# Conformer's last slice: two of its four blocks convolved by diagonal matmuls on TensorE, with the layer norm sums of the first three slices taken in the meantime

## The chip, the cores and the metric

The kernel runs as one program on one core of a Trainium2 chip. The metric is the device time of one execution in microseconds (us). The time of the kernel before is the median of 3 runs.

## The reference, cut to what matters

The model is a trunk of two layers over 256 tokens of width 2048 (batch 1). Layer 0 mixes tokens with a gated DeltaNet, layer 1 with a Conformer convolution module; each layer then applies a SwiGLU FFN. The change lies wholly in the Conformer module of layer 1:

```
def conformer_conv(h, pw1_w, pw1_b, dw_w, dw_b, ln_w, ln_b, pw2_w, pw2_b):
    u = h @ pw1_w + pw1_b                    # 2048 -> 4096
    a, gate = jnp.split(u, 2, axis=-1)
    u = a * jax.nn.sigmoid(gate)             # GLU, 2048 channels
    u = depthwise_conv(u, dw_w) + dw_b       # width 31, centred, over the 256 tokens
    u = jax.nn.silu(layernorm(u, ln_w, ln_b))# over the 2048 channels, LN_EPS = 1e-5
    return u @ pw2_w + pw2_b
```

`layernorm` subtracts the mean over the 2048 channels of a token, divides by the root of the mean square of what is left (plus LN_EPS), and applies a weight and a bias for each channel.

## The kernel before, in words

Each engine has its own instruction list, written out by hand (a `@block` function for each), and semaphores order the engines among themselves. No planner is involved: an instruction runs when those before it on its engine have been issued and its `wait_ge` is met.

**Layout.** In the Conformer the channels lie on the 128 partitions: the 2048 channels are 16 blocks (`kc`, KC = 16) of 128, the 256 tokens (T) lie along the free dimension. The work goes in four slices `n` of four blocks each. `glu` holds the four blocks of one slice after the GLU; `dwo` (a view of the buffer `y`, so rows of the profile call it y) holds all 16 blocks after the depthwise convolution. `psg`, `pst` and `psn` are PSUM buffers of 4, 2 and 2 banks.

**First projection (pw1).** TensorE multiplies the raw float32 weights (`tile32`, L630) for the two halves of a slice. ScalarE copies each half out of PSUM (`half`, L1915), TensorE transposes it (`turn2`, L620, called at L988 to L997), ScalarE takes the sigmoid (`sigm`, L1921), VectorE multiplies (`unit`, L1502). ScalarE has nothing else to do here: in this stage no weights are split. DMA brings one weight tile of 1 MB after the other into four slots.

**Depthwise convolution.** VectorE does it alone (`dw`, L1508 to L1526): 31 taps (`TAPS_V`, the centre tap first), for each tap one instruction for each of the four blocks. The first tap is a TENSOR_SCALAR with the bias (L1520), the 30 others are SCALAR_TENSOR_TENSOR, `dst = src * w + dst` (L1522). An instruction waits, by the semaphore `tap`, until the one four places before it has completed. The last instruction of a slice raises `dw_ok`. Slices 0 to 2 run in a loop, slice 3 (`dw(3, order)`, L1534) is written out.

**Layer norm.** Everything from here on waits for the fourth slice. TensorE sums over the channels by multiplying with a matrix of ones: 16 matmuls of 128 x 256 (L1004; the 12 of slices 0 to 2 can run early), VectorE divides by D (L1538) and subtracts the mean from all 16 blocks, four at a time (L1543), ScalarE squares four blocks at a time (L1943), TensorE sums the squares (L1009, 16 matmuls), VectorE divides (L1545), ScalarE takes the root (L1945), VectorE the reciprocal (L1547) and multiplies all blocks with it (L1551, four instructions).

**Second projection (pw2).** From here the kernel's matmuls use weights and activations split in a high and a low part: ScalarE makes `whi` (`hi`, L1596), VectorE `wlo` (`lo`, L1033), and `tile` (L643 and L649) does 16 matmuls with `whi` and 8 with `wlo` for a tile. VectorE makes `wlo` of the first two tiles between L1551 and L1556. ScalarE applies silu with weight and bias for each block (L1952) and copies to the high part `h_hi3` (L1956); VectorE subtracts to get the low part `h_lo3` (L1556) in four steps, and raises `pre_lo`, on which the first matmul of pw2 waits. Weights for the next slices of pw2 are loaded once `w_lo` tells that a slot is free. After pw2 come the residual update, the norm, and the FFN of layer 1.

Of the kernel before, what the change touches and what calls it, by code (L numbers as in the profile page):

```python
# [14 lines left out]
P = 128  # L15
D = 2048
T = 256
TT = T // P
KC = D // P
# [9 lines left out]
CTAPS = 31  # L29
TAPS_V = (CTAPS // 2,) + tuple(k for k in range(CTAPS) if k != CTAPS // 2)  # L30
# [4 lines left out]
RMS_EPS, LN_EPS, L2_EPS = 1e-6, 1e-5, 1e-6  # L35
# [29 lines left out]
def build(nc, x_in, c_in, ada_w, ada_b, norm_w, gdn_in_w, gdn_conv_w, gdn_A_log, gdn_dt_bias,  # L65
# [16 lines left out]
    G_P2 = G_P1 + 4 * 8  # L82
# [14 lines left out]
    with stack:  # L97
        def sb(name, shape, dt=F32, at=stack):
            return at.enter_context(nc.sbuf_tensor(name, shape, dt))

        def sem(name):
            return stack.enter_context(nc.semaphore(name))
# [19 lines left out]
        ident = sb("ident", [P, P])  # L122
        ones = sb("ones", [P, P])

        NV_NORM, NV_ADAB, NV_C, NV_CONV, NV_DW, NV_CF = 0, 128, 320, 336, 656, 1152
        vec = sb("vec", [P, 1232])
        V_PW1B, V_DWB, V_LNW, V_LNB = NV_CF, NV_CF + 32, NV_CF + 48, NV_CF + 64
# [94 lines left out]
        p3 = ExitStack()  # L222
        aring3 = sb("aring3", [P, 2, D], at=p3)
        aacc3 = sb("aacc3", [P, 2, D], at=p3)
        h_hi3 = sb("h_hi3", [P, KC, T], F32R, at=p3)
        h_lo3 = sb("h_lo3", [P, KC, T], F32R, at=p3)
        hf3 = sb("hf3", [P, 2, 4, T], at=p3)
# [10 lines left out]
        lnst = sb("lnst", [P, 2, T], at=p4)  # L238
        sg4 = sb("sg4", [P, 4, T], at=p4)
        glu = sb("glu", [P, 4, T], at=p4)  # L240
# [3 lines left out]
        h32 = aring3[:, :, :].rearrange("p a (k t) -> p (a k) t", t=T)  # L244
        pw2b = ev4[:, :, :, :].rearrange("p a t n -> p (a t n)")
        dwo = y[:, :, :].rearrange("p a (k t) -> p (a k) t", t=T)

        psg = stack.enter_context(nc.psum_tensor("psg", [P, 2, TT, NSL], F32))
        pst = stack.enter_context(nc.psum_tensor("pst", [P, 4, T], F32))
        psn = stack.enter_context(nc.psum_tensor("psn", [P, 4, T], F32))  # L250
# [43 lines left out]
        tap = sem("tap")  # L294
# [54 lines left out]

        ln_p, ln_v, ln_s = sem("ln_p"), sem("ln_v"), sem("ln_s")  # L350
        pb_land = sem("pb_land")
        out_sem = sem("out_sem")


# [261 lines left out]
        def _(pe):  # L616
            mm = nc.tensor.matmul
# [376 lines left out]
            with pe.Fori(1, 4) as i:  # L994
                pw1_pair(i, True)
            turn2((ps_read, S_P2), ev4[:, 1], psn, t_g, (sg_ok, 3))
            pe.wait_ge(sg_ok, 4)  # L997
            unsplit[0] = 32

            pe.wait_ge(glu_ok, 4)  # L1000
            for kc in range(KC):
                if kc % 4 == 0 and kc >= 8:
                    pe.wait_ge(dw_ok, kc // 4 + 1)
                i = mm(pst[:, 0, :], ones[:, :], dwo[:, kc, :], start=kc == 0, stop=kc == KC - 1)  # L1004
            i.then_inc(ln_p, 1)
            for q in range(4):
                pe.wait_ge(ln_s, q + 1)
                for j in range(4):
                    i = mm(pst[:, 2, :], ones[:, :], hf3[:, q % 2, j, :], start=q + j == 0, stop=q + j == 6)  # L1009
                i.then_inc(ln_p, 1)  # L1010
            with pe.Fori(0, 2) as i:
                for s in range(2):
                    n = 2 * i + s
                    pe.wait_ge(ps_read, S_P2 + n - 1)
                    for j in range(4):
                        tile(G_P2 + 4 * n + j, (G_P2 + j) % 2, psg[:, (S_P2 + s) % 2], h_hi3, h_lo3,
                             range(4 * j, 4 * j + 4), j == 0, j == 3, ready=(pre_lo, 8 + j + 1))
# [7 lines left out]
        def _(dve):  # L1025
# [482 lines left out]
            def dw(n, part):  # L1508

                for m, k in part:  # L1510
                    off = k - CTAPS // 2
                    a, e = max(0, -off), T - max(0, off)
                    for b in range(4):
                        if m:
                            dve.wait_ge(tap, dwt.at() - 3)
                        w = vec[:, ds(NV_DW + k * KC + 4 * n + b, 1)]
                        src = glu[:, b, a + off:e + off]
                        dst = dwo[:, ds(4 * n + b, 1), a:e].rearrange("p a t -> p (a t)")
                        if m == 0:
# [11 lines left out]
            with dwt.loop(dve, 1, 4, 4 * CTAPS - 1) as i:  # L1531
                pw1_pair(i)
            unit(3)
            dw(3, order)  # L1534

            lv = Tally(ln_v)
            dve.wait_ge(ln_p, 1)
            lv.inc(ts(lnst[:, 0, :], pst[:, 0, :], 1.0 / D, None, MUL))  # L1538
            lv.wait(dve)
            dve.wait_ge(dw_ok, 4)  # L1540
            for q in range(4):
                d4 = dwo[:, 4 * q:4 * q + 4, :]
                lv.inc(tt(d4, d4, lnst[:, 0:1, :].broadcast_to([P, 4, T]), SUB))  # L1543
            dve.wait_ge(ln_p, 5)
            lv.inc(ts(lnst[:, 1, :], pst[:, 2, :], 1.0 / D, LN_EPS, MUL, ADD))  # L1545
            dve.wait_ge(ln_s, 5)
            lv.inc(nc.vector.reciprocal(lnst[:, 1, :], lnst[:, 1, :]))  # L1547
            lv.wait(dve)
            for q in range(4):
                d4 = dwo[:, 4 * q:4 * q + 4, :]  # L1550
                lv.inc(tt(d4, d4, lnst[:, 1:2, :].broadcast_to([P, 4, T]), MUL))  # L1551
            for j in range(2):
                lo(G_P2 + j, G_P2 + j)
            for q in range(4):
                dve.wait_ge(ln_s, 5 + 2 * (q + 1))
                tt(h_lo3[:, 4 * q:4 * q + 4, :], hf3[:, q % 2], h_hi3[:, 4 * q:4 * q + 4, :].bitcast(F32),  # L1556
                   SUB).then_inc(pre_lo, 1)
            dve.wait_ge(pb_land, 16)

            def y_bias(n, par):  # L1560
# [27 lines left out]
        def _(act):  # L1588
# [37 lines left out]
            def pre(n, hi_, hfb, low0):  # L1626
                act.wait_ge(aff_ok, n + 1)

                def odd(q):

                    act.wait_ge(pre_tr, 4 * n + q + 1)
                    if q == 3 and hi_ is not None:
                        act.wait_ge(pre_lo, low0 + 2)
                    for j in range(4):
                        kc = 4 * q + j
                        i = av(hfb[:, kc, :] if hi_ is None else hfb[:, 1, j, :], psn[:, j, :], ACT.Identity, bias=mod[:, 3 * n, kc:kc + 1],
                               scale=aff[:, n, kc:kc + 1])
# [12 lines left out]
                odd(3)  # L1650
                high(3)
# [254 lines left out]
            ffn(0, G_F0, S_F0)  # L1906
            squares(2, lambda t: (x_up, 3 + t))
            pre(2, None, h32, 8)

            def half(n, which):  # L1910

# [24 lines left out]
            sigm(3)  # L1936
            hi(G_P2, G_P2)
            hi(G_P2 + 1, G_P2 + 1)
            for q in range(4):
                act.wait_ge(ln_v, 2 + q)  # L1940
                if q >= 2:
                    act.wait_ge(ln_p, q)
                av(hf3[:, q % 2], dwo[:, 4 * q:4 * q + 4, :], ACT.Square).then_inc(ln_s, 1)  # L1943
            act.wait_ge(ln_v, 6)
            av(lnst[:, 1, :], lnst[:, 1, :], ACT.Sqrt).then_inc(ln_s, 1)  # L1945
            for q in range(4):
                act.wait_ge(ln_v, 8 + q)
                if q >= 2:
                    act.wait_ge(pre_lo, 8 + q - 1)
                for j in range(4):  # L1950
                    kc = 4 * q + j
# [195 lines left out]
```

## Time and profile before

| | |
|---|---|
| median of 3 runs | 3355.26 us (3352.37 to 3358.61) |
| the profiled execution, its own time | 3356.01 us |
| its span | 3354.4 us |
| mean granted TensorE clock | 0.947 of full speed |
| busy: TensorE matmul / weight load | 2975.1 us (89%) / 2390.3 us (71%) |
| busy: VectorE | 2319.3 us (69%) |
| busy: ScalarE | 1255.6 us (37%) |
| busy: GpSimd | 249.6 us (7%) |

The profile describes one execution. PE is TensorE's matmul and PEld its weight load, DVE is VectorE, ACT is ScalarE, POOL is GpSimd, SP is the engine that issues most DMAs. L12 is line 12 of the kernel. A float32 matmul shows as two records: the 12 early matmuls of L1004 are 24 of them. The record of a matmul runs on beyond the start of the next one, so what a stream of them costs is read from the time of the whole stream and its count. The granted clock (PEclk) is 1.00 at 2.4 GHz and 0.50 at 1.2 GHz.

### The profile page before, as it was taken

The page shows a single profiled execution, that of the slowest core. Times are in us where ns is not written, and L with a number is a line of the kernel's source. Part 1 is how long each engine was busy: PE and PEld are TensorE (multiplying, and loading weights), DVE is VectorE, ACT ScalarE, POOL GpSimd, SP SyncE. Part 2 cuts the span into 40 slices and gives each one's busy share as a digit, 9 for nine tenths or more (in the row PEclk, how much of TensorE's full clock was granted, in tenths as well). Part 3 has the DMA queues.
Part 4 walks back from the last instruction along what each step waited for, and adds up shares of the span by engine and source line. Part 5 has one row for each costly group of instructions (what it writes and reads, how often), then busy time and mean ns, then how long its engine had stood idle before and what let it go on. Part 6 is the DMA issues. An engine that isn't in the chain of part 4 may idle for free.

```text
span 3354.4 us, 37695 instructions
## 1 busy us (share of the span) xinstructions
PE 2975.1 (89%) x13446; PEld 2390.3 (71%) x13446; DVE 2319.3 (69%) x2367; ACT 1255.6 (37%) x1143; POOL 249.6 (7%) x266
## 2 busy tenths in 40 slices
PE   1599999997778599799999999799757999999998
PEld 1578878876667478688888888644346788888886
DVE  7588868976767377787877878529965655565555
ACT  0256644334454433433333333301134433333333
POOL 0011111323333100000000000000000000000000
PEclk9899999998999699899999999899878999999998
DMA  9467766664332299688978888354324666665663
GB/s 361 179 225 239 241 211 230 204 221 140 97 97 82 56 382 361 250 315 315 343 291 313 329 317 333 122 163 151 113 74 164 238 201 204 214 206 201 201 212 125
DMA packets 322154, 731.34 MB, mean 218 GB/s; under 512 B 48129, under 2 KB 64337, under 8 KB 293649
## 3 DMA queue, kind: packets, MB, share of 16 engines
q1 hardware_dynamic: 316256, 709.85, 60.0%
q0 software_dynamic: 5808, 20.35, 1.8%
q8 instruction: 50, 0.82, 0.1%
q14 instruction: 40, 0.32, 0.0%
HBM read 710.45 MB, written 19.69 MB: 218 GB/s over the span
## 4 chain that ended last, share of the span: by engine, by line
PE 78%; DVE 11%; ACT 4%; DMA 3%; issue 3%; DVEq 1%; SPq 0%; POOL 0%; ACTq 0%; POOLq 0%
PE psg L643 43%; PE psg L649 21%; PE psg L630 5%; DVE y L1522 2%; DMA aring<-in_ada_w 2%; PE pst L809 1%; PE psn L670 1%; DVE exb L1373 1%; PE pst L620 1%; ACT dec L1790 1%; DMA wraw<-in_gdn_out_w 1%; DVE wlo L1033 1%; DVE aacc L1137 1%; PE psn L620 1%; PE pst L802 1%
## 5 line engine op out<-in xcount | busy, mean ns | idle before, releaser
L1033 DVE TENSOR_TENSOR wlo<-wraw,whi 128x2048 fp32r<-128x2048 f32 x409 | 937.2, 2292 | 488.2 <-ACT whi L1596 486.4
L1596 ACT ACTIVATE whi<-wraw 128x2048 fp32r<-128x2048 f32 x409 | 783.5, 1916 | 1307.4 <-PE psg L649 1201.5
L643 PE MATMUL psg<-whi,h_hi 128*128 128x512 f32 (+1 forms) x2336 | 742.2, 400 | 35.5 <-DVE h_lo L1556 13.0
L643 PE MATMUL psg<-whi,h_lo 128*128 128x512 f32 (+1 forms) x2336 | 731.4, 395 | 0.0
L649 PE MATMUL psg<-wlo,h_hi 128*128 128x512 f32 (+1 forms) x2336 | 582.6, 393 | 12.1 <-DVE wlo L1033 12.1
L643 PEld LDWEIGHTS psg<-whi,h_hi 128*128 128x128 f32 x2336 | 445.2, 194 | 130.2 <-issue 21.0
L649 PEld LDWEIGHTS psg<-wlo,h_hi 128*128 128x128 f32 x2336 | 443.0, 191 | 104.8 <-DVE wlo L1033 13.8
L643 PEld LDWEIGHTS psg<-whi,h_lo 128*128 128x128 f32 x2336 | 449.1, 193 | 94.1
L1043 DVE SCALAR_TENSOR_TENSOR aacc<-aring,cond,aacc 128x2048 f32<-128x2048 f32 x151 | 354.2, 2345 | 6.7 <-DMA aring<-in_ada_w 6.0
L630 PE MATMUL psg<-wraw,aring 128*128 128x512 f32 x512 | 221.1, 592 | 0.0
L643 PE MATMUL psg<-whi,g_hi 128*128 128x512 f32 x704 | 219.9, 394 | 0.0
L643 PE MATMUL psg<-whi,g_lo 128*128 128x512 f32 x704 | 219.4, 393 | 0.0
L1522 DVE SCALAR_TENSOR_TENSOR y<-glu,vec,y 128x241 f32 (+29 forms) x480 | 186.4, 462 | 0.0
L630 PEld LDWEIGHTS psg<-wraw,aring 128*128 128x128 f32 x512 | 96.7, 190 | 118.6 <-issue 118.6
L649 PE MATMUL psg<-wlo,g_hi 128*128 128x512 f32 x704 | 173.9, 389 | 0.0
L2079 POOL DMA_DIRECT2D d_cw<-cwc x4 | 4.7, 1172 | 2123.1 <-DVE cwc L1117 2123.1
L643 PEld LDWEIGHTS psg<-whi,g_hi 128*128 128x128 f32 x704 | 134.1, 191 | 28.0
L643 PEld LDWEIGHTS psg<-whi,g_lo 128*128 128x128 f32 x704 | 133.9, 190 | 28.2
L1441 DVE TENSOR_TENSOR y<-psg,y 128x1024 f32<-128x1024 f32 x88 | 107.5, 1222 | 66.9 <-PE psg L649 65.7
L649 PEld LDWEIGHTS psg<-wlo,g_hi 128*128 128x128 f32 x704 | 132.2, 188 | 27.5
L1236 DVE SCALAR_TENSOR_TENSOR cv<-pst,vec,cv 128x254 f32<-128x254 f32 (+1 forms) x256 | 117.2, 480 | 25.1 <-DVE cv L1234 0.2
L670 PE MATMUL psn<-ones,aacc 128*128 128x1 f32 x384 | 57.9, 285 | 81.5 <-DVE aacc L1137 48.6
(216 smaller groups left out, 2650.7 us busy)
## 6 DMA issues: line engine op xcount, KB each, us to landing
aring<-in_ada_w SPq DMA_DIRECT2D x192, 1024.0 KB, 7.0
wraw<-in_ffn_in_w SPq DMA_DIRECT2D x176, 1024.0 KB, 6.8
wraw<-in_gdn_in_w SPq DMA_DIRECT2D x97, 1024.0 KB, 5.2
wraw<-in_ffn_out_w SPq DMA_DIRECT2D x88, 1024.0 KB, 5.4
wraw<-in_cf_pw_w SPq DMA_DIRECT2D x48, 1024.0 KB, 5.3
wraw<-in_gdn_out_w SPq DMA_DIRECT2D x32, 1024.0 KB, 8.8
wraw<-d_rr SPq DMA_DIRECT2D x16, 1024.0 KB, 5.1
x<-in_x SPq DMA_DIRECT2D x2, 2048.0 KB, 9.9
```

The source lines that it names most:

```text
L620: return nc.tensor.transpose(dst, src, ident[:, :])
L630: i = mm(ps[:, t, :], a[:, kc, t * P:(t + 1) * P], wraw[:, slot, j * NSL:(j + 1) * NSL], start=first and j == 0, stop=last and j == len(kc ...
L643: mm(ps[:, t, 0:width], a[:, kc, t * P:(t + 1) * P], wh, start=first and j + n == 0, stop=False)
L649: i = mm(ps[:, t, 0:width], a_hi[:, kc, t * P:(t + 1) * P], wl, start=False, stop=last and j == len(kcs) - 1)
L670: i = mm(psn[:, 0, kc:kc + 1], acc[:, kc * P:(kc + 1) * P], ones[:, 0:1], start=True, stop=True)
L802: i = mm(ps_a[:, c, :], t64[:, q, c, t, :], rv[:, q, o, c, :], start=True, stop=True)
L1033: tt(wlo[:, j % 2, :], wraw[:, j % 4, :], whi[:, j % 2, :].bitcast(F32), SUB).then_inc(w_lo, 1)
L1043: stt(acc, ring[:, par, :], c, acc, MUL, ADD).then_inc(a_used, 1)
L1236: i = stt(dst, src, w, dst, MUL, ADD)
L1441: tt(yj, psg[:, (s0 + par) % 2], yj, ADD).then_inc(ps_read, 1)
L1522: i = stt(dst, src, w, dst, MUL, ADD)
L1596: av(whi[:, j % 2, :], wraw[:, j % 4, :], ACT.Copy).then_inc(w_hi, 1)
```

## The change

- A buffer `diag` of 2 x 32 matrices of 128 x 128 floats, laid over `h_hi3` and `h_lo3`, which are unused between the FFN of layer 0 and pw2. ScalarE fills 62 of them right after the input of the Conformer module is normed (`pre(2, ...)`): the identity times a column of tap weights, for the 31 taps of blocks 14 and 15.
- Slice 3 on VectorE (`dw_last`) does only blocks 12 and 13: 62 instructions where there were 124, each waiting for the one two places before. Blocks 14 and 15 are convolved on TensorE: 62 float32 matmuls of a diagonal matrix with `glu` shifted by the tap, accumulated in two banks of `psn`; ScalarE takes them out with the bias.
- TensorE takes the 12 mean sums of slices 0 to 2 before the diagonal matmuls, as soon as `dw_ok` reaches 3, so it no longer waits for the last GLU there. After tap 16 VectorE computes from them a provisional mean over 1536 channels (`mean0`) and subtracts it from the 12 blocks, then finishes the taps and subtracts it from the other four. ScalarE squares the first three slices during the taps, TensorE sums their squares after the diagonal matmuls, then sums the four blocks of slice 3 and its squares.
- The mean of the shifted blocks is now that of slice 3's four blocks divided by D (those of the first three slices sum to nought after the shift). The variance is the mean square of the shifted values less the square of that mean (`dev2`). The mean is subtracted (`center`) together with the scaling, block group by block group.
- `lo` of the first pw2 tile moves ahead of the wait for TensorE's blocks; that of the second behind the first `h_lo3` step.

```diff
@@ tensor @@
             turn2((ps_read, S_P2), ev4[:, 1], psn, t_g, (sg_ok, 3))
+            unsplit[0] = 32
+            pe.wait_ge(dw_ok, 3)
+            for kc in range(12):
+                i = mm(psg[:, 0, 0, 0:T], ones[:, :], dwo[:, kc, :], start=kc == 0, stop=kc == 11)
+            i.then_inc(ln_p, 1)
             pe.wait_ge(sg_ok, 4)
-            unsplit[0] = 32
-
             pe.wait_ge(glu_ok, 4)
-            for kc in range(KC):
-                if kc % 4 == 0 and kc >= 8:
-                    pe.wait_ge(dw_ok, kc // 4 + 1)
-                i = mm(pst[:, 0, :], ones[:, :], dwo[:, kc, :], start=kc == 0, stop=kc == KC - 1)
-            i.then_inc(ln_p, 1)
-            for q in range(4):
+            pe.wait_ge(diag_ok, 1)
+            for m, k in enumerate(TAPS_V):
+                off = k - CTAPS // 2
+                a, e = max(0, -off), T - max(0, off)
+                for b in range(2):
+                    i = mm(psn[:, 2 * b, a:e], diag[:, b, m, :], glu[:, 2 + b, a + off:e + off], start=m == 0, stop=m == CTAPS - 1)
+            i.then_inc(dwp_done, 1)
+
+            def square_sums(q):
                 pe.wait_ge(ln_s, q + 1)
                 for j in range(4):
-                    i = mm(pst[:, 2, :], ones[:, :], hf3[:, q % 2, j, :], start=q + j == 0, stop=q + j == 6)
+                    i = mm(psg[:, 1, 1, 0:T], ones[:, :], lnsq[:, q, j * T:(j + 1) * T], start=q + j == 0, stop=q + j == 6)
                 i.then_inc(ln_p, 1)
+            for q in range(3):
+                square_sums(q)
+            pe.wait_ge(ln_v, 6)
+            for j in range(4):
+                i = mm(psg[:, 1, 0, 0:T], ones[:, :], dwo[:, 12 + j, :], start=j == 0, stop=j == 3)
+            i.then_inc(ln_p, 1)
+            square_sums(3)
@@ vector @@
-            dw(3, order)
+            def dw_last(part):
+                for m, k in part:
...
+                    for b in range(2):
+                        if m:
+                            dve.wait_ge(tap, dwt.at() - 1)
...
             lv = Tally(ln_v)
+            mean0, dev2 = sg4[:, 0:1, :], sg4[:, 1, :]
+            def shift(k0, n):
+                lv.inc(tt(dwo[:, k0:k0 + n, :], dwo[:, k0:k0 + n, :], mean0.broadcast_to([P, n, T]), SUB))
+            dw_last(order[:16])
             dve.wait_ge(ln_p, 1)
-            lv.inc(ts(lnst[:, 0, :], pst[:, 0, :], 1.0 / D, None, MUL))
+            lv.inc(ts(sg4[:, 0, :], psg[:, 0, 0, 0:T], 1.0 / (12 * P), None, MUL))
             lv.wait(dve)
+            for q in range(3):
+                shift(4 * q, 4)
+            dw_last(order[16:])
             dve.wait_ge(dw_ok, 4)
+            shift(12, 2)
+            lo(G_P2, G_P2)
+            dve.wait_ge(dwp_ok, 1)
+            shift(14, 2)
+            dve.wait_ge(ln_p, 5)
+            lv.inc(ts(lnst[:, 0, :], psg[:, 1, 0, 0:T], 1.0 / D, None, MUL))
+            lv.wait(dve)
+            lv.inc(tt(dev2, lnst[:, 0, :], lnst[:, 0, :], MUL))
+            lv.wait(dve)
+            lv.inc(ts(dev2, dev2, -1.0, LN_EPS, MUL, ADD))
...
+            center(0)
+            dve.wait_ge(ln_p, 6)
+            lv.wait(dve)
+            lv.inc(stt(lnst[:, 1, :], psg[:, 1, 1, 0:T], 1.0 / D, dev2, MUL, ADD))
             dve.wait_ge(ln_s, 5)
             lv.inc(nc.vector.reciprocal(lnst[:, 1, :], lnst[:, 1, :]))
             lv.wait(dve)
-            for q in range(4):
-                d4 = dwo[:, 4 * q:4 * q + 4, :]
-                lv.inc(tt(d4, d4, lnst[:, 1:2, :].broadcast_to([P, 4, T]), MUL))
-            for j in range(2):
-                lo(G_P2 + j, G_P2 + j)
+            scale(0)
+            for q in range(1, 4):
+                center(q)
+                lv.wait(dve)
+                scale(q)
...
+            low(0)
+            lo(G_P2 + 1, G_P2 + 1)
+            for q in range(1, 4):
+                low(q)
@@ scalar @@
             pre(2, None, h32, 8)
+            for b in range(2):
+                for m, k in enumerate(TAPS_V):
+                    c = NV_DW + k * KC + 14 + b
+                    i = av(diag[:, b, m, :], ident[:, :], ACT.Copy, scale=vec[:, c:c + 1])
+            i.then_inc(diag_ok, 1)
...
-            for q in range(4):
+            def square(q):
+                av(lnsq[:, q, :], dwo[:, 4 * q:4 * q + 4, :].rearrange("p k t -> p (k t)"), ACT.Square).then_inc(ln_s, 1)
+            for q in range(3):
                 act.wait_ge(ln_v, 2 + q)
-                if q >= 2:
-                    act.wait_ge(ln_p, q)
-                av(hf3[:, q % 2], dwo[:, 4 * q:4 * q + 4, :], ACT.Square).then_inc(ln_s, 1)
+                square(q)
+            act.wait_ge(dwp_done, 1)
+            for b in range(2):
+                i = av(dwo[:, 14 + b, :], psn[:, 2 * b, :], ACT.Identity, bias=vec[:, V_DWB + 14 + b:V_DWB + 15 + b])
+            i.then_inc(dwp_ok, 1)
             act.wait_ge(ln_v, 6)
+            square(3)
+            act.wait_ge(ln_v, 11)
             av(lnst[:, 1, :], lnst[:, 1, :], ACT.Sqrt).then_inc(ln_s, 1)
             for q in range(4):
-                act.wait_ge(ln_v, 8 + q)
+                act.wait_ge(ln_v, 13 + 2 * q)
```

`center(q)` subtracts the mean from four blocks and `scale(q)` multiplies them by the reciprocal root; each is one VectorE instruction of 128 x 1024.

## Rows read from the trace of the kernel before

**Rows 1.** The page: the chain that ended last, shares by engine and line.
```profile
PE 78%; DVE 11%; ACT 4%; DMA 3%; issue 3%; DVEq 1%; SPq 0%; POOL 0%; ACTq 0%; POOLq 0%
```

**Rows 2.** That chain in order of time, 2402 to 2520: start, length, what (xcount).
```profile
2404.49 1.67 DVE glu L1502 x4
2406.19 1.38 DVE y L1520 x4
2407.57 46.51 DVE y L1522 x120
2454.12 3.70 PE pst L1004 x8
...
2459.57 1.07 ACT hf L1943
2460.67 8.88 PE pst L1009 x32
2469.57 0.44 DVE lnst L1545
2470.03 0.42 ACT lnst L1945
2470.48 1.76 DVE lnst L1547
2472.27 4.63 DVE y L1551 x4
2476.90 4.40 DVE wlo L1033 x2
2481.30 1.15 DVE h_lo L1556
...
2482.58 6.56 PE psg L643 x16
2489.14 1.81 PE psg L649 x8
2490.96 3.63 PE psg L643 x16
```

**Rows 3.** Timeline of PE around the last GLU: start, length, group, [idle before <-releaser].
```profile
2401.33 1.09 PE L620 MATMUL psn<-ident,ev 128*128 128x128 f32 x8 [1.11 <-ACT ev L1915]
2406.30 7.11 PE L1004 MATMUL pst<-y,ones 128*128 128x256 f32 x24 [3.88 <-DVE glu L1502]
```

**Rows 4.** Windows: length, busy (xcount) of PE, PEld, DVE, ACT, POOL, then PEclk, DMA.
```profile
2406.00:2410.00 4.00, 3.70 (x9) 3.00 (x10) 3.96 (x12) 1.62 (x1) 0.00 (x0) 0.57 0.29 121
2410.00:2414.00 4.00, 3.40 (x16) 2.66 (x14) 4.00 (x12) 0.00 (x0) 0.00 (x0) 1.00 0.00 0
```

**Rows 5.** Timeline of PE elsewhere: small float32 matmuls, and the pause before one group.
```profile
1109.72 2.92 PE L893 MATMUL psn<-wraw,dec 128*128 128x128 f32 x24 [0.84 <-DVE og L1366]
2109.07 3.62 PE L670 MATMUL psn<-ones,aacc 128*128 128x1 f32 x32
804.38 1.16 PE L809 MATMUL pst<-yh,dec 128*128 128x128 f32 x8 [2.03 <-ACT yh L1781]
```

**Rows 6.** Window just after that pause, same columns as Rows 4.
```profile
806.00:808.00 2.00, 2.00 (x8) 1.36 (x7) 1.97 (x4) 0.00 (x0) 2.00 (x3) 0.50 0.01 4
```

**Rows 7.** Timeline of ACT: before pw1, and the operations that the change's new ones resemble.
```profile
2156.57 0.20 ACT L1624 ACTIVATE st<-st 128x2 f32<-128x2 f32 x1
2174.39 1.93 ACT L1636 ACTIVATE aring<-psn,mod,aff 128x256 f32<-128x256 f32 x4 [1.18 <-PE psn L620]
2201.85 1.02 ACT L1915 ACTIVATE ev<-psg 128x1024 f32<-128x1024 f32 x1 [25.54 <-PE psg L630]
2473.53 2.08 ACT L1952 ACTIVATE hf<-y,vec 128x256 f32<-128x256 f32 x4 [1.78 <-DVE y L1551]
```

**Rows 8.** Timeline of PE: the transposes that use the first half of pw1.
```profile
2208.52 1.04 PE L620 MATMUL pst<-ident,ev 128*128 128x128 f32 x8
```

**Rows 9.** Timeline of DVE: a conv chain waiting tap by tap; a 512 element add.
```profile
291.84 3.92 DVE L1236 SCALAR_TENSOR_TENSOR cv<-pst,vec,cv 128x254 f32<-128x254 f32 x8
2511.53 1.28 DVE L1563 TENSOR_TENSOR y<-psg,ev 128x512 f32<-128x512 f32 x2
```

More of the change, by code:

```diff
@@ L224, in build @@
         aacc3 = sb("aacc3", [P, 2, D], at=p3)
+        p3d = ExitStack()
+        diag = sb("diag", [P, 2, 32, P], at=p3d)
+        p3d.close()
         h_hi3 = sb("h_hi3", [P, KC, T], F32R, at=p3)
@@ L246, in build @@
         dwo = y[:, :, :].rearrange("p a (k t) -> p (a k) t", t=T)
+        lnsq = aacc3[:, :, :].rearrange("p a (q n) -> p (a q) n", q=2)
         psg = stack.enter_context(nc.psum_tensor("psg", [P, 2, TT, NSL], F32))
@@ L351, in build @@
         pb_land = sem("pb_land")
+        diag_ok, dwp_done, dwp_ok = sem("diag_ok"), sem("dwp_done"), sem("dwp_ok")
         out_sem = sem("out_sem")
@@ L1533, in _ @@
             unit(3)
-            dw(3, order)
+            def dw_last(part):
+                for m, k in part:
+                    off = k - CTAPS // 2
+                    a, e = max(0, -off), T - max(0, off)
+                    for b in range(2):
+                        if m:
+                            dve.wait_ge(tap, dwt.at() - 1)
+                        w = vec[:, NV_DW + k * KC + 12 + b:NV_DW + k * KC + 13 + b]
+                        src, dst = glu[:, b, a + off:e + off], dwo[:, 12 + b, a:e]
+                        if m == 0:
+                            i = ts(dst, src, w, vec[:, V_DWB + 12 + b:V_DWB + 13 + b], MUL, ADD)
+                        else:
+                            i = stt(dst, src, w, dst, MUL, ADD)
+                        if m == CTAPS - 1 and b == 1:
+                            i.then_inc(dw_ok, 1)
+                        else:
+                            dwt.inc(i)
@@ L1540, in _ @@
+            dw_last(order[16:])
             dve.wait_ge(dw_ok, 4)
-            for q in range(4):
+            shift(12, 2)
+            lo(G_P2, G_P2)
+            dve.wait_ge(dwp_ok, 1)
+            shift(14, 2)
+            assert lv.n == 6
+            dve.wait_ge(ln_p, 5)
[4 more added lines that the diff above has]
+            lv.inc(ts(dev2, dev2, -1.0, LN_EPS, MUL, ADD))
@@ L1542, in _, with center, scale @@
+            def center(q):
                 d4 = dwo[:, 4 * q:4 * q + 4, :]
                 lv.inc(tt(d4, d4, lnst[:, 0:1, :].broadcast_to([P, 4, T]), SUB))
-            dve.wait_ge(ln_p, 5)
-            lv.inc(ts(lnst[:, 1, :], pst[:, 2, :], 1.0 / D, LN_EPS, MUL, ADD))
+            def scale(q):
+                d4 = dwo[:, 4 * q:4 * q + 4, :]
+                lv.inc(tt(d4, d4, lnst[:, 1:2, :].broadcast_to([P, 4, T]), MUL))
+            center(0)
+            dve.wait_ge(ln_p, 6)
+            lv.wait(dve)
@@ L1546, in _ @@
+            lv.inc(stt(lnst[:, 1, :], psg[:, 1, 1, 0:T], 1.0 / D, dev2, MUL, ADD))
+            assert lv.n == 11
             dve.wait_ge(ln_s, 5)
@@ L1548, in _, with low @@
             lv.wait(dve)
-            for q in range(4):
-                d4 = dwo[:, 4 * q:4 * q + 4, :]
-                lv.inc(tt(d4, d4, lnst[:, 1:2, :].broadcast_to([P, 4, T]), MUL))
-            for j in range(2):
-                lo(G_P2 + j, G_P2 + j)
-            for q in range(4):
+            scale(0)
[3 more added lines that the diff above has]
+                scale(q)
+            def low(q):
                 dve.wait_ge(ln_s, 5 + 2 * (q + 1))
@@ L1938, in _ @@
             hi(G_P2 + 1, G_P2 + 1)
-            for q in range(4):
+            def square(q):
+                av(lnsq[:, q, :], dwo[:, 4 * q:4 * q + 4, :].rearrange("p k t -> p (k t)"), ACT.Square).then_inc(ln_s, 1)
+            for q in range(3):
                 act.wait_ge(ln_v, 2 + q)
-                if q >= 2:
-                    act.wait_ge(ln_p, q)
-                av(hf3[:, q % 2], dwo[:, 4 * q:4 * q + 4, :], ACT.Square).then_inc(ln_s, 1)
+                square(q)
[3 more added lines that the diff above has]
+            i.then_inc(dwp_ok, 1)
             act.wait_ge(ln_v, 6)
+            square(3)
+            act.wait_ge(ln_v, 11)
             av(lnst[:, 1, :], lnst[:, 1, :], ACT.Sqrt).then_inc(ln_s, 1)
             for q in range(4):
-                act.wait_ge(ln_v, 8 + q)
+                act.wait_ge(ln_v, 13 + 2 * q)
                 if q >= 2:
```

## The prediction

> **What bounds the kernel now.** I read the page's chain of waits first, then that chain in order of time, then the timelines of the engines and the windows with the granted clock. Over the whole span TensorE carries 78% of the chain and VectorE 11% [rows 1]. Around the change it is the other way round. From the last GLU (2404.49) to the first matmul of pw2 (2482.58) lie 78.1 us, in which VectorE's 120 tap instructions alone hold 46.51 us; then come four mean sums (3.70), the subtraction, squares and their sums (8.88), root and reciprocal, the scaling (4.63), two weight splits (4.40) and the first low part (1.15) [rows 2]. TensorE does 12 early sums at 2406.30 and then has nothing until 2454.12 [rows 2, 3]. After 2482.58 the chain is TensorE, tile by tile (3.63 + 1.81 us), so I take what the first pw2 matmul gains as a gain of the whole kernel, all later work keeping its distance to it.
>
> **Where the 12 sums go.** They now wait for slice 2, not for the last GLU. TensorE's transposes end at 2402.42 [rows 3] and VectorE leaves slice 2 just before it starts the GLU at 2404.49 [rows 2]; I take 2404.45. The stream of 24 records took 7.11 us [rows 3], of which the first part ran at clock 0.57 and the rest at 1.00 [rows 4]. At full clock 16 records take 3.40 us, 0.2125 each [rows 4], and 24 would take 5.10. Whether the clock still falls when TensorE pauses 2.0 us instead of 3.88 is open. After a pause of 2.03 us elsewhere it did fall: the granted clock was 0.50 right after [rows 5, 6]. I take the fall and 7.0 us: the sums end at 2411.45. Without it they end 1.9 us sooner; both ends stay in the range.
>
> **The diagonal matmuls.** 62 matmuls are 124 records. The taps shorten the moving side: 31 x 256 less 2 x (1 + ... + 15) is 7,696 columns a block, 15,392 in all, or 30,784 counted twice, which is 120.25 records of 256. At 0.2125 [rows 4] that is 25.55 us. The nearest rows: L1004 is the same operation in the same size, and loads weights before each record too, but always the same ones; L893 has other weights each time and 128 columns, and takes 2.92 / 24 = 0.122 a record [rows 5], against 0.106 for half of 0.2125. The surplus of 0.016 x 124 = 2.0 us is one bound, part of it the end of the last record. Nothing here excludes a gain from the clock staying up, counted above. I take 25.55, since L1004 is nearest in size. So the diagonals end at E = 2437.0.
>
> No row has a moving operand that starts at an odd element, as the shifted `glu` does. The bounds are no cost and the half clock pitch (below); I take none.
>
> The weight load is where a rule of the Trainium skill speaks against the change ("TensorE: Matmul & The Clock Gate", section "LDWEIGHTS (loading the stationary operand)"): a load takes the number of its columns divided by 1.2 in ns, so 107 ns for 128, and the section "Back-to-back issue gap" lets both operations set the spacing. An estimate from that page with nothing hidden would be 124 x 0.107 = 13.3 us on top; with the load pulled ahead of running matmuls it is none. The trace bears out the second, since L1004's 0.2125 holds a load as well.
>
> **VectorE meanwhile.** After the GLU (2406.19) the first tap is two instructions of 1.38 / 4 = 0.345, the next 15 taps are 30 of 46.51 / 120 = 0.388: 2418.5 [rows 2]. The wait for the 12 sums (2411.45) is over. The provisional mean costs 0.46, three subtractions of 128x1024 3 x 1.16 (4.63 / 4 [rows 2]): 2422.4. 30 more taps: 2434.1. The subtraction of two blocks is about 0.64 (1.28 / 2 [rows 9]), the weight split 2.2 (4.40 / 2 [rows 2]): 2437.0, level with E. Waiting for the one two places back is bounded below by 0.388, as now, and above by 3.92 / 8 = 0.49, where a two block chain waits for all of the tap before [rows 9]; that would be 60 x 0.10 = 6 us. I take 0.388: two places are 0.78 us, and the instruction's own length is under 0.5.
>
> ScalarE squares three slices at 2420 to 2424 with nothing else queued. It takes TensorE's blocks out at E: two at 1.93 / 4 = 0.48 [rows 7], till E + 1.0. VectorE subtracts from them till E + 1.7, ScalarE squares till E + 2.8. Queued behind VectorE's wait for `dwp_ok` is all the statistics; they wait for TensorE longer anyway: it first sums 12 squares (24 records, 5.1 us) to E + 5.1. This cover is 3.4 us wide; with VectorE at 0.49 a tap it is gone and costs 1.8.
>
> **From E to pw2.** TensorE: mean sums of slice 3, 8 records, E + 6.8; its squares, E + 8.5. VectorE: mean 0.46, its square 0.45 and the third 0.37: E + 8.1; `center(0)` complete at E + 9.3 (the last sum came at E + 8.5); the variance 0.48, root 0.46, reciprocal 1.78 [rows 2]: E + 12.05. Then `scale(0)`, and three times `center` and `scale`; where one follows freely it is 1.16, where `scale` waits for `center` 1.27: `low(0)` starts at E + 12.07 + 4 x 1.16 + 3 x 1.27 = E + 20.5. ScalarE's silu and high part of the first four blocks (2.08 [rows 7] and 1.07) are done by E + 16.5. `low(0)` ends at E + 21.7 and TensorE starts at E + 21.9. Before, the same stretch from the reciprocal's end was 4.63 + 4.40 + 1.15; now it is 9.7: three centrings in, two weight splits out.
>
> So pw2 starts at 2437.0 + 21.9 = 2458.9 instead of 2482.58: 23.7 us sooner.
>
> **Is it given back?** The moved split of tile 1 runs E + 21.7 to E + 24.0, and its `wlo` and second low part (E + 25.1) are needed when tile 0 is through, 8.38 us after the start (2482.58 to 2490.96 [rows 2]), at E + 30.3. The fourth low part waits twice for its buffer, done by E + 29.5, needed after two more tiles. SP's load of the fifth pw2 tile comes 20 us sooner, that of the sixth 2 us after pw2's start; both are needed 20 us later. TensorE pauses 13.4 us before pw2 where it paused 13.05, so pw2's slow first tile (8.38 instead of 5.44) stays.
>
> **Building the diagonals.** ScalarE is free from 2176.3 until 2201.85 [rows 7]. One costs between 0.20 (128x2) and 0.48 (128x256 [rows 7]); I take 0.34, so 62 take 21.1 us, till 2197.4. At the upper end it is 29.8, till 2206.1: then the copy of the first half is late, but TensorE wants it only at 2208.52 [rows 8] and the copy takes 1.02. The cover holds at both ends: no cost.
>
> **The sum.** The profiled execution took 3356.01 us (span 3354.4 and 1.6 around it). Less 23.7 that is 3332.3. The runs' median lies 0.75 below it, so I forecast 3331.6. The forecast's own range is 3328 to 3337: clock that does not fall (-1.9), the surplus of L893 (+2.0), VectorE's slower taps (+1.8), and some 2 us by which the medians of this kernel move.
>
> **Rivals.**
> - *Weight loads of new diagonals are not hidden.* A record of one column is nearly all weight load: 3.62 / 32 = 0.113 [rows 5]. In series that adds 124 x 0.113 = 14.0 us: 3345.6. Against it: L893's 0.122 for a load and 128 columns is far below the 0.219 that a series would take. 5%.
> - *The clock stays at half through the diagonals.* Sums 10.2, diagonals 51.1, E at 2465.8; the five groups of sums after it take twice as long too, so pw2 starts near E + 29.7 = 2495.5, 12.9 us later than before: 3368. The same mechanism can come from slow reads of shifted columns. It decides from the point where a record of 256 columns takes over (2460.7 - 2411.45) / 120.25 = 0.41 us: then E passes 2460.7 and nothing is gained. For it: the clock falls here after short pauses [rows 4 to 6]. Against: it came back within the 12 sums [rows 4]. 4%.
> - *Partial failure by a wait I have mis-ordered or an engine that interferes* (VectorE and ScalarE beside TensorE in this stretch), 5 to 12 us of the gain lost: 3337 to 3344. For it: three engines hand over five times between E and pw2. Against: each handover in the present chain costs 0.02 to 0.04 us beside the work. 9%.
> - *The change doesn't do what it says*: the gain is eaten by later waits for weights, as the end of the kernel is TensorE with its own loads. Time as before, 3355. Nothing in the rows after pw2 speaks for it. 2%.
>
> **Chances.** Forecast 80%, the rivals 5, 4, 9 and 2%. The range that holds it 8 times in 10 is 3327 to 3343. About 0.2%, 6.7 us, is what a measurement of this kernel can tell from no change. The first rival and nearly all of the third are still faster by more: faster 0.93, same 0.03, slower 0.04.
>
> **What would show it.** In the changed profile: 62 ACT instructions of the diagonals ending before 2207; PE busy without a gap from about 2404.5 to 2445, at a clock of 1.00 after the first 5 us; 124 records in 25.6 us; DVE taps at 0.388 with one break of 4 us; the first L643 of pw2 21.9 us after the last diagonal, near 2459. Wrong if the diagonal records stand over 0.23 apart, if VectorE and not TensorE releases the mean sums of slice 3, or if the distance from pw2's start to the end (871.8 us in the span before) changes by more than 2 us.

## The result: 0.9% faster, and more than forecast

| | before | changed |
|---|---|---|
| median, first comparison | 3353.82 us (4 runs, 3348.51 to 3358.61) | 3323.66 us (4 runs, 3317.95 to 3325.32) |
| ratio, 95% interval | | 0.9907 (0.9888 to 0.9927) |
| profiled execution, its own time / span | 3356.01 / 3354.4 us | 3324.57 / 3322.9 us |
| clock, mean over the span | 0.947 | 0.954 |

The forecast was 3331.6 us in a range from 3327 to 3343. The measured time lies 3.3 us below that range. The sign was right, and the mechanism inside the changed stage came out as forecast; what was off is told below.

The page after, the chain's shares by engine and the busy slices of TensorE and its clock (an answer to [rows 1]):

```profile
PE   1599999997787599799999999899987999999998
PEclk9899999998999699899999999899998999999998
...
PE 80%; DVE 9%; ACT 4%; DMA 3%; issue 3%; DVEq 1%; SPq 0%; POOL 0%; ACTq 0%; POOLq 0%
```

The chain in order of time, from the end of slice 2's taps to pw2 (start, length, what), is to be laid beside [rows 2]. The GLU starts at 2400.45; it isn't on the chain any more.

```profile
2399.10 1.22 DVE y L1541 x3
...
2400.37 5.45 PE psg L1006 x24
2405.82 25.96 PE psn L1015 x124
2431.78 5.18 PE psg L1021 x24
2436.96 1.74 PE psg L1027 x8
...
2438.72 0.44 DVE lnst L1592
2439.18 0.43 DVE sg L1594
2439.64 0.29 DVE sg L1596
2439.93 1.14 DVE y L1600
...
2441.18 0.44 DVE lnst L1608
...
2442.09 1.76 DVE lnst L1611
2443.87 1.22 DVE y L1604
...
2451.06 1.23 DVE y L1604
2452.29 1.15 DVE h_lo L1621
...
2453.57 5.48 PE psg L648 x16
```

The 46.51 us of taps are gone from it. TensorE holds it without a gap from the 12 sums (L1006) over the 124 records of the diagonals (L1015) and the square sums (L1021) to the mean sums of slice 3 (L1027); then comes VectorE's tail. From the GLU's start to pw2's start it is 53.12 us, where it was 78.09: 24.97 us gained.

The DVE timeline of the same stretch (start, length, group, what ended the idle time before) shows why VectorE is off the chain until 2438.72: its taps keep their pace of 0.39 us with two in flight (11.71 us for 30), and then it waits 5.18 us for TensorE's mean sums. The ACT timeline shows the diagonals built in 18.2 us, with 7.46 us left before the next copy.

```profile
2402.80 11.71 DVE L1567 SCALAR_TENSOR_TENSOR y<-glu,vec,y 128x241 f32<-128x241 f32 x30
2414.44 0.42 DVE L1580 TENSOR_SCALAR sg<-psg 128x256 f32<-128x256 f32 x1
2414.89 3.50 DVE L1577 TENSOR_TENSOR y<-y,sg 128x1024 f32<-128x1024 f32 x3
2418.30 11.71 DVE L1567 SCALAR_TENSOR_TENSOR y<-glu,vec,y 128x255 f32<-128x255 f32 x30
...
2438.72 0.42 DVE L1592 TENSOR_SCALAR lnst<-psg 128x256 f32<-128x256 f32 x1 [5.18 <-PE psg L1027]
```

```profile
2172.16 18.20 ACT L1981 ACTIVATE diag<-ident,vec 128x128 f32<-128x128 f32 x62
2197.81 1.02 ACT L1989 ACTIVATE ev<-psg 128x1024 f32<-128x1024 f32 x1 [7.46 <-PE psg L635]
```

The two spans differ by 31.45 us, so 6.5 us lie outside the stage: 4.04 us before it (the GLU starts at 2400.45, not 2404.49) and 2.44 us after it (869.36 us from pw2's start to the end, not 871.80). The prediction had named a change of more than 2 us in that last distance as a sign of being wrong; this sign came. The question of the experiments is whether these belong to the change.

### The profile page after: what moved, and what is told of

The parts are those of the page before. It is cut to its first block, busy times and chain, and to the rows that moved or that the text cites. A ratio compares the mean times of both kernels' runs of the same rounds, so it can differ in the third digit from the quotient of the medians.

```text
span 3322.9 us, 37951 instructions
## 1 busy us (share of the span) xinstructions
PE 2991.6 (90%) x13570; PEld 2406.8 (72%) x13570; DVE 2302.0 (69%) x2313; ACT 1274.6 (38%) x1207; POOL 249.6 (8%) x266
## 4 chain that ended last, share of the span: by engine, by line
PE 80%; DVE 9%; ACT 4%; DMA 3%; issue 3%; DVEq 1%; SPq 0%; POOL 0%; ACTq 0%; POOLq 0%
PE psg L648 44%; PE psg L654 22%; PE psg L635 5%; DMA aring<-in_ada_w 2%; PE psn L675 1%; PE pst L814 1%; DVE exb L1392 1%; PE pst L625 1%; ACT dec L1859 1%; DMA wraw<-in_gdn_out_w 1%; DVE wlo L1052 1%; DVE aacc L1156 1%; PE psn L1015 1%; DVE y L1541 1%; PE psn L625 1%
## 5 line engine op out<-in xcount | busy, mean ns | idle before, releaser
L648 PEld LDWEIGHTS psg<-whi,h_hi 128*128 128x128 f32 x2336 | 444.6, 193 | 130.0 <-issue 21.1
L1541 DVE SCALAR_TENSOR_TENSOR y<-glu,vec,y 128x242 f32 (+14 forms) x360 | 139.8, 463 | 0.0
```

The source lines that it names most:

```text
L648: mm(ps[:, t, 0:width], a[:, kc, t * P:(t + 1) * P], wh, start=first and j + n == 0, stop=False)
```

## The experiments

Theory A: the change gives what the stage shows, and the rest is what one execution differs from the next. Rival B: the other 5 to 6.5 us come from the change too. Twelve runs were made, three of them repeats of the changed kernel or the kernel before and two of them repeats of experiments. They ran in three batches (e1 to e4, e5 to e8, e9 to e12), each batch on one chip, beside the kernel before. Read from each trace: the start of the last GLU, the stage (GLU to pw2), the 12 sums with TensorE's pause before them, pw2's first tile, one group of the FFN (the first after a pause of 3 us, about 130 us behind pw2's start), and the distance from pw2's start to the end.

| kernel | GLU | stage | pause, 12 sums | first tile | FFN group | to the end | ratio of times (95%) |
|---|---|---|---|---|---|---|---|
| before | 2404.49 | 78.09 | 3.88, 7.11 | 8.21 | 3.35 | 871.80 | |
| changed | 2400.45 | 53.12 | 1.99, 5.45 | 7.13 | 1.95 | 869.36 | 0.9907 (0.9888 to 0.9927) |
| e1 before again | 2400.69 | 78.02 | 3.88, 7.07 | 8.19 | 3.32 | 871.72 | 1.000 (0.999 to 1.001) |
| e2 changed again | 2400.36 | 53.11 | 1.99, 5.45 | 7.12 | 1.98 | 869.32 | 0.9924 (0.9909 to 0.994) |
| e3 diagonals only | 2407.75 | 61.49 | 3.88, 7.10 | 7.98 | 3.58 | 871.45 | 0.9952 (0.9939 to 0.9964) |
| e4 sums only | 2395.39 | 73.47 | 1.98, 7.13 | 8.39 | 3.43 | 872.13 | 0.9982 (0.9972 to 0.9991) |
| e5 sums late | 2399.52 | 56.61 | 3.83, 7.10 | 7.08 | 1.96 | 869.30 | 0.9932 (0.9919 to 0.9946) |
| e6 centre early | 2397.17 | 49.64 | 1.99, 5.45 | 7.09 | 1.98 | 869.33 | 0.9903 (0.9887 to 0.9918) |
| e7 centre early, warm | 2394.90 | 49.63 | 1.99, 5.45 | 5.53 | 3.52 | 869.31 | 0.9895 (0.988 to 0.991) |
| e8 warm | 2401.28 | 53.11 | 1.99, 5.45 | 5.56 | 3.44 | 869.29 | 0.9919 (0.9905 to 0.9932) |
| e9 changed, third | 2401.85 | 53.10 | 1.99, 5.45 | 7.09 | 1.95 | 869.28 | 0.9922 (0.9909 to 0.9935) |
| e10 centre early again | 2394.44 | 52.18 | 1.99, 8.15 | 7.62 | 3.58 | 870.86 | 0.991 (0.9897 to 0.9923) |
| e11 before, warm | 2396.08 | 79.55 | 3.87, 8.41 | 5.55 | 3.51 | 869.25 | 0.9991 (0.9982 to 1.0) |
| e12 sums only again | 2399.33 | 73.48 | 1.99, 5.45 | 7.13 | 1.95 | 869.43 | one run |

**Both kernels again, unchanged: e1, e2 and e9.** No edit.

> The kernel before, unchanged, run again as if it were a candidate, so that its trace and its times show how much one execution differs from the next outside the changed stage. Theory A (of the 31.4 us between the two spans, about 25 to 26 belong to the Conformer's last slice and the first tile behind it; the 4.0 us gained before it, in the DeltaNet stage near 771 us, and part of what was gained after it are chance): here the last GLU starts up to 4 us away from 2404.49 although nothing was changed, the stage from GLU to the first matmul of pw2 is 78.1 us again within 0.3, and the median ratio to the kernel before is 1.000. Rival B (the other 5 to 6 us come from the change too, by placement of code or by another order of the DMAs): the GLU starts at 2404.5 within 1 us again.

> The changed kernel, unchanged, again. Theory A: the stage from the last GLU to the first matmul of pw2 is 53.1 us again (within 2, by the clock in the 12 sums), and the gain in the median against the kernel before is 25 to 27 us. Rival B: the gain is 30 to 31 us again with the stage at 53.1, and the GLU starts 4 us sooner than in the kernel before.

> The changed kernel a third time, on the same chip as the kernel with the early centrings. Theory A (the change's own share is the stage, 25.0 us, and 2.5 us of granted clock behind it; the rest of the first comparison was scatter before the GLU): stage 53.1 us, GLU somewhere between 2395 and 2408 us, gain in the median 25 to 28 us. Rival B: gain 30 us or more.

The kernel before, run again, started its GLU 3.80 us sooner than it had, with nothing changed: rival B's mark, 2404.5 within 1 us, isn't met. The changed kernel repeated its stage to 0.02 us. Its gain came out as 0.9924 and 0.9922. Times the medians of the kernel before (3347.57 us in 23 runs, 3350.65 in 17) that is 25.4 us (20 to 30) and 26.1 us (22 to 30), where theory A said 25 to 27 for e2 and 25 to 28 for e9; the 30 us and more of rival B lie at the edge of both intervals. The first comparison, 31 us, has 25 to 26 inside its interval (24 to 38 us). Over all 14 traces the GLU starts between 2394.44 and 2407.75, kernels with and without the change mixed: the mean is 2399.3 in the eleven with the change or a part of it and 2400.4 in the three without. In the kernel before there was a wait for the last DMA to `d_z`, which stands in the chain near 760 us in eleven of the 14 traces. It took 7.86 us in the changed kernel and 9.83 in the one before, which looked like rival B; in the changed kernel's third trace it took 11.20. These are that row of the chain before, then in the third trace of the changed kernel, then in e1:

```profile
761.09 9.83 DMA d_z<-zw
```

```profile
758.34 11.20 DMA d_z<-zw
```

```profile
760.63 10.51 DMA d_z<-zw
```

This wait isn't the whole of the scatter either. In the kernel before the data has landed at 770.92 and in its repeat e1 at 771.14, and yet e1's GLU starts 3.80 us sooner: that difference arises later on. In the eleven traces the landing moves between 766.03 and 771.14, and the distance from it to the GLU between 1626.2 and 1633.6 us.

**One part of the change alone: e3, e4 and e12.** e3 is the kernel before with

```diff
+                if kc == 12:
+                    pe.wait_ge(diag_ok, 1)
+                    ...   # the 62 diagonal matmuls, then dwp_done
                 if kc % 4 == 0 and kc >= 8:
                     pe.wait_ge(dw_ok, kc // 4 + 1)
+                if kc == 14:
+                    pe.wait_ge(dwp_ok, 1)
@@ vector @@
-            dw(3, order)
+            dw_last(order)
```

and ScalarE's building and taking out of blocks 14 and 15. e4 and e12 are the changed kernel with

```diff
-            pe.wait_ge(diag_ok, 1)
-            ...   # the 62 diagonal matmuls, their building and taking out
@@ vector, in dw_last @@
-                for m, k in part: ...
+                dw(3, part)
```

> The kernel before with the diagonal matmuls alone: layer norm as before, the 12 early sums still behind the last GLU. If the terms add up as the trace says: DVE's taps end 24 us after the GLU's products, TensorE's 12 sums (7.1 us if the clock falls, 5.5 if not) and 124 records (26.0) end about 33 to 35 us after the GLU starts, then evacuation, 4 sums, subtraction, squares and sums as before: pw2 starts 60 to 62.5 us after the GLU, a gain of 16 to 18 us. Rival (the two edits only pay together, since the layer norm then stands whole behind the diagonals): a gain under 12 us.

> The changed kernel without the diagonals: VectorE does all four blocks' taps, but the mean sums, the provisional mean and the squares of the first three slices are taken meanwhile. VectorE's taps are then longer by the shift of 12 blocks in their middle (3.9 us), behind them 8 us of subtraction, squares and sums go, centrings come in, and TensorE is at half clock again after its pause. Expected: pw2 starts 74 to 76 us after the GLU, a gain of 2 to 4 us. Rival (the early layer norm is most of the gain): over 8 us.

> The kernel with the early sums and no diagonals again, for one question: its TensorE paused 1.98 us before the 12 sums, as in the changed kernel, and yet the clock fell in them (7.13 us against 5.45 in all five traces with the diagonals and the sums moved). If that is chance, it may be 5.45 here; if it belongs to the kernel, 7.1 again.

e3: the stage is 61.49 us, 16.6 less than before, ratio 0.9952. The chain of e3:

```profile
2409.55 7.10 PE pst L1019 x24
2416.65 25.98 PE psn L1012 x124
...
2442.66 0.85 ACT y L1981 x2
...
2443.55 1.15 PE pst L1019 x4
...
2447.54 8.66 PE pst L1024 x32
```

The diagonals alone are two thirds of the gain, and after them the layer norm stands whole. e4: 73.47, 4.6 less, a little more than expected (2 to 4), ratio 0.9982. Alone they give 16.6 + 4.6 = 21.2 us, together 25.0. Two things are true of the two together and of neither alone. The shift in the middle of the taps (3.50 us) is off the chain, because TensorE sets it. And the early place of the 12 sums is on it, worth 3.5 us by e5 below, of which 1.65 us is clock; in e4 and e12 the sums took 7.13 and 5.45 us and the stage was 73.47 and 73.48, so without the diagonals their length is worth nothing. How the 3.8 us divide between the two isn't shown. e12 is e4's kernel again, and answers another question: its 12 sums took 5.45 us after the pause of 1.99 us, where e4's took 7.13 after 1.98. The PE timelines of e4 and then of e12:

```profile
2395.30 7.13 PE L1002 MATMUL psg<-y,ones 128*128 128x256 f32 x24 [1.98 <-DVE y L1530]
```

```profile
2399.24 5.45 PE L1002 MATMUL psg<-y,ones 128*128 128x256 f32 x24 [1.99 <-DVE y L1530]
```

**The sums' place: e5.**

```diff
-            pe.wait_ge(dw_ok, 3)
-            ...   # the 12 mean sums
             pe.wait_ge(sg_ok, 4)
             pe.wait_ge(glu_ok, 4)
+            pe.wait_ge(dw_ok, 3)
+            ...   # the 12 mean sums
             pe.wait_ge(diag_ok, 1)
```

> The changed kernel with the 12 sums behind the last GLU again, as they were. Their pause before is then 3.9 us, before which the clock fell in each trace so far (7.1 us for the 24 records against 5.45 in the changed kernel). Theory (moving the sums gives 2.0 us of start and, as long as the clock stays up, 1.65 of clock): the diagonals end 3.6 us later, VectorE is then 1.9 us less on the path, stage from GLU to pw2 56.5 to 57 us instead of 53.1, the gain against the kernel before about 3.5 us smaller. Rival (the sums' place is covered by VectorE, which ends 2433.5 beside TensorE's 2431.8): stage under 54.5 us. If the clock falls in neither, 55.0.

The PE timeline of e5:

```profile
2401.28 7.10 PE L1008 MATMUL psg<-y,ones 128*128 128x256 f32 x24 [3.83 <-DVE glu L1521]
```

The stage is 56.61 us, 3.5 more than 53.11, as expected to the tenth. The sums start 1.84 us later, counted from the GLU's start, and the sums take 1.65 us longer, at the clock that had fallen. TensorE is the bound: VectorE didn't cover it. The timed ratio, 0.9932 beside 0.9922 and 0.9924, goes the same way but is within the intervals, so this size rests on the traces.

**A better order behind the diagonals: e6 and e10.**

```diff
-            for q in range(3):
-                square_sums(q)
+            square_sums(0)
             pe.wait_ge(ln_v, 6)
             ...   # slice 3's mean sums
-            square_sums(3)
+            for q in range(1, 4):
+                square_sums(q)
@@ vector @@
-            center(0)
+            dve.wait_ge(ln_s, 4)
+            for q in range(4):
+                center(q)
...
-            scale(0)
-            for q in range(1, 4):
-                center(q)
-                lv.wait(dve)
-                scale(q)
+            for q in range(4):
+                scale(q)
```

with the waits counted anew.

> The changed kernel with another order behind the diagonals: TensorE takes slice 3's mean sums after the first square sums instead of after the third, and VectorE does all four centrings while TensorE sums squares, so that only the four scalings stand between the reciprocal and the first low part. From the trace of the changed kernel: 8.38 us from the reciprocal's end to the end of the scalings become 4.64, minus up to 0.1 us that the variance starts later. Expected: stage 49.3 to 49.7 us instead of 53.1, gain 3.6 us larger. Rival (ScalarE's silu and high part of the first blocks, 3.2 us behind the first scaling, become the last wait): stage 50.5 or more.

> The kernel with the early centrings again, beside the changed kernel: stage 49.6 us, 3.4 to 3.5 us faster than the changed kernel, in the ratios to the kernel before about 0.001.

The chain of e6:

```profile
2429.65 0.61 DVE y L1577
...
2430.31 2.01 PE psg L1026 x8
...
2433.55 4.55 DVE y L1600 x4
...
2438.20 0.44 DVE lnst L1610
...
2440.90 4.63 DVE y L1604 x4
2445.53 1.15 DVE h_lo L1620
...
2446.81 3.33 PE psg L648 x7
```

The stage is 49.64, 3.5 us shorter, and the medians are 3318.44 and 3320.56 us, where the changed kernel had 3324.2 and 3325.76. That is clearly faster than the kernel before; against the changed kernel the times point the same way, but the intervals overlap (on one chip 0.991, 0.9897 to 0.9923, beside e9's 0.9922, 0.9909 to 0.9935), so the 3.5 us rest on the trace. The centrings (L1600) run beside the square sums, and ScalarE's silu isn't the last wait (the rival). In e6 it is VectorE whose last subtraction (L1577) releases the mean sums, about 0.1 us after TensorE is done with the first square sums: the two engines end level. The second run missed its stage: 52.18 instead of 49.6, because the clock fell in its 12 sums, which took 8.15 us after the same pause. The windows over these sums in e10 and then in e6 (length, busy, granted clock, DMA share, GB/s) show it:

```profile
2394.00:2397.00 3.00, 2.65 (x6) 0.50 1.00 406
2397.00:2400.00 3.00, 3.00 (x9) 0.52 0.04 16
```

```profile
2397.00:2400.00 3.00, 2.91 (x14) 1.00 0.89 367
2400.00:2403.00 3.00, 3.00 (x15) 1.00 0.06 25
```

**The clock behind the pause: e7, e8 and e11.** Behind the last sums, e7 (on e6), e8 (on the changed kernel) and e11 (on the kernel before, into `psn` from `h32`) have

```diff
+            for j in range(29):   # 20 in e7
+                mm(pst[:, 0, :], ones[:, :], lnsq[:, j % 4, 0:T], start=True, stop=True)
```

> The kernel with the early centrings, and 20 extra matmuls of 128x256 behind the last sums, whose result nobody reads, so that TensorE doesn't pause before pw2. Theory (the first tiles of pw2 are slow, 7.1 to 8.4 us instead of 5.44, only because of the granted clock after the pause): the first tile takes 5.5 us, the rest of the kernel after pw2's start is 1.5 to 2.9 us shorter than 871.8, if the matmuls end before pw2 can start (8.5 us in a pause of about 9.5). Rival (the first tile is slow by its operands' arrival): unchanged at 7 to 8 us.

> The changed kernel with 29 extra matmuls of 128x256 behind the last sums (12.4 us in the pause of 13.2), nobody reads them. Theory of the clock: first tile of pw2 5.5 us, gain 1.5 to 2.9 us larger than the changed kernel's; start of pw2 unchanged at 53.1 us after the GLU. Also a further sample of what lies outside the stage: theory A (chance) expects the landing of the last DMA to d_z and the distance from pw2's start to the end to scatter here as they did with the unchanged kernels; rival B expects 4 us less before the GLU in each kernel with the change.

> The kernel before with 29 extra matmuls of 128x256 behind the layer norm's sums, whose result nobody reads, in the pause of 13 us before pw2. If the 2.5 us that the changed kernel gains behind pw2's start are the granted clock in pw2's first tile and in one group of the FFN, this kernel shows the first tile at 5.5 us instead of 8.2, and 869.3 us or 871.8 less 2.7 from pw2's start to the end, with the kernel's taps and layer norm as before (stage 78.1). If they come from the change in another way: 871 to 872.

In all three pw2's first tile takes 5.5 us: it was slow by the clock alone. But e7 gained nothing by it on e6, and e8 nothing on the changed kernel, against what I expected of e8 (their ratios, 0.9895 and 0.9919, are inside the intervals of those kernels): the distance to the end stayed at 869.3. e7's mark, 1.5 to 2.9 us below 871.8, was met, but e6 without the extra matmuls had met it already. The group of the FFN behind a pause of 3 us took 3.4 to 3.5 us instead of 1.95, and so the 1.6 us were given back. The PE timelines of the changed kernel and then of e8:

```profile
2584.86 2.11 PE L654 MATMUL psg<-wlo,h_hi 128*128 128x512 f32 x8 [3.00 <-DVE wlo L1052]
```

```profile
2584.10 3.60 PE L654 MATMUL psg<-wlo,h_hi 128*128 128x512 f32 x8 [2.96 <-DVE wlo L1054]
```

e11 shows what the expectation asked: with the old taps and the old layer norm, 869.25 us from pw2's start to the end. So the 2.44 us after pw2 need nothing of the change. Yet they came in all three traces of the changed kernel (869.28 to 869.36) and in neither of the two of the kernel before (871.72, 871.80), so whether the change favours them stays open. What they are is clock: first tile and FFN group together are 11.56 us in the kernel before, 9.08 in the changed one, 9.06 in e11, 11.82 in e4 and 9.08 in e12, which is e4's kernel. The table shows one thing more: the FFN group is fast (1.95 to 1.98 us) in just the six traces whose first tile took 7.08 to 7.13 us, and slow (3.32 to 3.58) in the other eight; what ties the two isn't shown. e11's stage was 79.55, 1.5 longer, nearly all of it in the square sums, 10.21 us instead of 8.86, with the granted clock at 0.50 from 2452 to 2458. Its 12 early sums took 8.41 us, but they aren't on the chain.

```profile
2452.37 10.21 PE L1009 MATMUL pst<-hf,ones 128*128 128x256 f32 x32 [2.87 <-ACT hf L1945]
```

## Why the prediction was wrong, by its own steps

The step that failed is the level that the forecast starts from. The prediction took 3355.26 us, the median of three runs, and allowed for "some 2 us by which the medians of this kernel move"; the medians of later batches were 3.7 to 7.7 us lower. The gain itself was mis-sized by less: 23.7 us forecast, 25.4 and 26.1 measured. The changed kernel's medians of 3324.20 and 3325.76 us in the later batches lie below 3327 as well.

Term by term, in the two traces of the first comparison: the changed kernel's span should have been 3330.7 us and was 3322.93. The 7.8 us are:

- **Where the 12 sums go: 1.6 us.** The prediction had them over at 6.96 us after the GLU's start, with the clock fallen; they were over at 5.37. It had named this end ("Without it they end 1.9 us sooner") and chosen the other, because one pause of 2.03 us elsewhere had been followed by half clock. In nine traces with a pause of 2 us here the clock held in seven and fell in two, and the same kernel stands on both sides twice (e4 and e12, e6 and e10). After 3.8 to 3.9 us it fell in five of five. The likelier end was the other one.
- **The diagonals: -0.4 us.** 25.96 us for 124 records, not 25.55. New weights for each matmul and odd starts cost at most that 0.4; the rivals of the unhidden load and of half clock didn't come up. In the Trainium skill ("TensorE: Matmul & The Clock Gate") the section "LDWEIGHTS (loading the stationary operand)" gives 107 ns for loading 128 columns, an estimate of 13 us for 124 loads if nothing hid them; the section "Step-by-step: what each phase is for" has the next weights load while a matmul runs. The trace, with 0.209 us a record, bears out the second.
- **VectorE meanwhile: right.** The second taps end 29.6 us after the GLU's start, as forecast; the first weight split is over at 32.4 (32.5).
- **From E, the end of the diagonals, to pw2: 0.1 us.** 21.79 us, not 21.9.
- **"pw2's slow first tile (8.38 instead of 5.44) stays": 1.1 us, and the FFN group 1.4.** This sentence failed. I had counted the pause's length and taken the loss as fixed. The granted clock was 0.50 for the first 5.7 us of pw2 in the kernel before and for the first 3.3 us in the changed one, which makes the first tile 1.1 us shorter (8.38 and 7.29 us by the chain); at the group in the FFN it was down in one and up in the other.
- **Building the diagonals: right**, 18.2 us at 0.29 each (forecast 21.1 at 0.34), hidden.
- **What lies before the GLU: 4.0 us**, whose instructions are the same apart from the building of the diagonals, which is hidden. Together with the level this is what broke the range: "some 2 us by which the medians of this kernel move". One execution's GLU starts up to 13.3 us from another's, and the medians of the kernel before were 3355.26 (3353.82 with a fourth run), 3347.57, 3351.52 and 3350.65 us. The forecast of the gain, 23.7 us, is inside both later intervals (20 to 30 and 22 to 30 us), and just outside the first (24 to 38). The forecast of the time stood on a median of three runs that was the highest of the four, with room for 2 us where 4 to 8 were needed. That the first comparison's own gain, 31 us, lies above the later two is put down to the same scatter; it isn't shown run by run.

What stays open: what decides whether the clock holds over a pause of 2 us, and why in e7 and e8 the 1.6 us won at pw2's first tile were lost at the FFN group. Where the 13 us before the GLU arise is open as well: the DMA to `d_z` (7.65 to 11.20 us) is one place, more arises behind it, and neither was tested.

## What to carry to other kernels

Where one engine does a chain of cheap instructions of one kind and another stands idle, cut the chain so that both end together, and move the next stage's sums into the time won: here both together gave 3.8 us more than the sum of each alone, because the first part decides which engine the second is hidden behind. After such a move ask again what stands between the last long wait and the next stage; the order of mean, centring and scaling was worth 3.5 us more in the stage. When a time is forecast from few runs, give the level of the kernel its own share of the range; when a gain is forecast, compare on one chip.

## What the runs showed of the hardware

- A float32 matmul with a diagonal of 128 x 128 and 241 to 256 shifted columns takes 0.42 us (two records of 0.209), with other weights each time; VectorE's tap takes 0.39. The two engines ran at these paces beside each other in all nine traces with the diagonals.
- The same kernel with the same pause of 1.98 to 1.99 us keeps TensorE's clock in one execution (e12, e6) and loses it in another (e4, e10), which makes its 12 sums 1.7 to 2.7 us longer (5.45 against 7.13 and 8.15).
- Keeping TensorE busy through a pause of 9 to 13 us brings the next tile to full speed (5.5 us instead of 7.1 to 8.4), but in e7 and e8 the time to the end was the same (869.3 us), since a loss of 1.5 us came up at the next pause of 3 us; in e11, where that group had been slow anyway, 2.5 us were gained.
